# Experts' weights with adjacent rows on each partition, router and filter steps reordered, in a two-block hybrid layer with a mixture of experts

## The reference, cut to what matters

```python
probs = softmax(h @ router_w); sel = probs + router_b
idx = top 2 of sel inside the best of 4 groups of experts
gp = probs[idx] / sum(probs[idx])
for e in range(16):
    he = (silu(h @ w_gate[e]) * (h @ w_up[e])) @ w_down[e]   # 1024x512, 1024x512, 512x1024
    out = out + combine[:, e:e+1] * he
x = x + gate * out
return rmsnorm(x, final_norm_g)
```

## Time and profile before

| | |
|---|---|
| median of 3 runs | 1018.84 us (1018.74 to 1019.75) |
| profiled execution, its own time | 1019.72 us |
| its span | 1017.9 us |
| PE busy | 963.6 us (95%) |
| DVE, ACT, POOL busy | 619.0, 458.8, 53.7 us |
| DMA | 229.71 MB, 226 GB/s over the span |
| mean granted PE clock | 0.987 |

### The profile page before, as it was taken

One profiled execution on the slowest core, in us unless ns is written; L12 is line 12 of the kernel. 1 busy time (PEld: TensorE's weight loads), 2 busy tenths in 40 slices (PEclk: granted clock), 3 DMA queues, 4 the chain that ended last, 5 costly groups with the idle time before them and its releaser, 6 DMA issues.

```text
span 1017.9 us, 14807 instructions
## 1 busy us (share of the span) xinstructions
PE 963.6 (95%) x6088; PEld 743.2 (73%) x6088; DVE 619.0 (61%) x1085; ACT 458.8 (45%) x739; POOL 53.7 (5%) x74
## 2 busy tenths in 40 slices
PE   9989998999998989999989999999799999999994
PEld 6778676778897979999877886899775555544541
DVE  5666639587637476576564899665952545472725
ACT  4576742976645464344653101336640324252402
POOL 0200000000000000000010312000000000010120
PEclk9999999999999999999989999999999999999997
DMA  9933877875342754524461134001799999999992
GB/s 327 246 135 131 280 249 253 290 277 199 132 166 84 272 183 153 180 83 169 165 198 56 67 126 166 1 1 66 274 405 363 404 395 392 409 405 403 399 411 112
DMA packets 111313, 229.71 MB, mean 226 GB/s; under 512 B 8518, under 2 KB 16999, under 8 KB 111246
## 3 DMA queue, kind: packets, MB, share of 16 engines
q1 hardware_dynamic: 107966, 219.40, 59.5%
q0 software_dynamic: 2992, 8.79, 2.2%
q10 hardware_dynamic: 288, 0.58, 0.2%
HBM read 221.01 MB, written 7.74 MB: 225 GB/s over the span
## 4 chain that ended last, share of the span: by engine, by line
PE 65%; DVE 21%; ACT 6%; DMA 4%; issue 3%; SPq 0%; DVEq 0%; ACTq 0%
PE bank L1731 8%; PE bank L2856 8%; PE bank L1732 7%; PE bank L1733 7%; PE bank L956 5%; PE bank L2802 4%; PE bank L2803 3%; PE bank L2804 3%; PE bank L2880 3%; PE bank L907 3%; DMA slot<-in_moe_w_down 2%; DVE slot_rounded L1721 1%; DMA arena<-in_ctxT 1%; PE bank L1159 1%; DVE slot_rounded L772 1%
## 5 line engine op out<-in xcount | busy, mean ns | idle before, releaser
L1731 PE MATMUL bank<-rounded 128*128 128x256 f32 (+1 forms) x800 | 245.7, 307 | 13.4 <-DVE slot_rounded L1721 5.9
L1732 PE MATMUL bank<-rounded 128*128 128x256 f32 x704 | 199.2, 283 | 0.0
L1733 PE MATMUL bank<-rounded,slot_rounded 128*128 128x256 f32 x624 | 176.8, 283 | 0.0
L1731 PEld LDWEIGHTS bank<-rounded 128*128 128x128 f32 x800 | 152.3, 190 | 32.5 <-issue 16.5
L1732 PEld LDWEIGHTS bank<-rounded 128*128 128x128 f32 x704 | 134.4, 191 | 1.0 <-issue 0.7
L1733 PEld LDWEIGHTS bank<-rounded,slot_rounded 128*128 128x128 f32 x624 | 119.3, 191 | 0.0
L956 PE MATMUL bank<-x_and_h,slot 128*128 128x256 f32 x416 | 93.7, 380 | 1.4 <-ACT x_and_h L652 1.4
L1721 DVE TENSOR_TENSOR slot_rounded<-slot,rounded 128x1024 fp32r<-128x1024 f32 (+1 forms) x72 | 74.1, 1052 | 32.1 <-ACT rounded L1715 31.9
L956 PEld LDWEIGHTS bank<-x_and_h,slot 128*128 128x128 f32 x416 | 77.8, 190 | 13.2 <-issue 3.0
L1715 ACT ACTIVATE rounded<-slot 128x1024 fp32r<-128x1024 f32 (+1 forms) x72 | 63.3, 908 | 25.1 <-PE bank L1733 25.1
L1010 ACT ACTIVATE arena<-bank 128x256 f32<-128x256 f32 x56 | 21.5, 385 | 99.2 <-PE bank L956 69.6
(11 more groups left out here) (511 smaller groups left out, 1926.3 us busy)
## 6 DMA issues: line engine op xcount, KB each, us to landing
slot<-in_w_in SPq DMA_DIRECT2D x26, 2048.0 KB, 8.4
slot<-in_ada_w SPq DMA_DIRECT2D x12, 2048.0 KB, 8.4
slot<-in_moe_w_down SPq DMA_DIRECT2D x10, 2048.0 KB, 18.3
more_slots<-in_moe_w_gate SPq DMA_DIRECT2D x8, 2048.0 KB, 15.7
more_slots<-in_moe_w_up SPq DMA_DIRECT2D x8, 2048.0 KB, 18.6
slot<-in_moe_w_gate SPq DMA_DIRECT2D x7, 2048.0 KB, 12.0
more_slots<-in_moe_w_down SPq DMA_DIRECT2D x5, 2048.0 KB, 17.1
x_and_h<-in_moe_w_up SPq DMA_DIRECT2D x5, 2048.0 KB, 15.2
```

The lines of the kernel that those rows point to most:

```text
L1731: t.do.matmul(dst, w_hi, x_hi, start=start, stop=False)
L1732: t.do.matmul(dst, w_hi, x_lo, start=False, stop=False)
L1733: return t.do.matmul(dst, w_lo, x_hi, start=False, stop=stop)
```

## The change

Weights: a partition now holds 8 adjacent rows of a gate or up matrix (4 of a down matrix), 16 KB in one run of DRAM, where it held rows 128 apart. Channel `c` then sits on partition `c // 8`, place `c % 8`, so tokens are put in that order: transposes and gathers take every eighth column of the token tiles as the stationary operand, `turn` every fourth of the hidden rows, and a quad's gate and up products read every fourth column of the weights. Gain and shift are put in that order by a PE transpose and a trip through DRAM (`gain_turn`). Order: ranks are turned by a PE product, compared, and multiplied with the token numbers on PE. Gathers of the first quarter start with token tile 0, and the second half of `tokens_low` moves behind `onehot(0)`; ACT's first `split`s and DVE's third `gathered` change places with their neighbours. Filter: layer 0 one channel job earlier, and two channel jobs more between layer 1 and the taps; POOL's cast waits for the last angle, the ones are filled by DVE. Attention: `weigh` behind `cmp_keys`, one `mix` behind `ada` 6. Tail: the first token tile's picks are added ahead of the last two blocks' rows; the fetch of the second tile and the final row wait for the last weights; squares by halves; the second half's gain and root in one operation.

```diff
-        PLAN += [*channels("f0")[0:2], *woven([*channels("f0")[2:], *channels("f1"), *channels("q2")], taps)]
+        PLAN += [pf0[0], pf0[1], taps[0], pf0[2], pf0[3], taps[1], pf1[0], pf1[1], *woven([*pf1[2:], *pq2], taps[2:])]
+        for job, behind in ((("weigh", ("slc", 0, 1)), ("cmp_keys",)), (("mix", ("slc", 0, 0)), ("ada", 6))):
+            PLAN.remove(job)
+            PLAN.insert(PLAN.index(behind) + 1, job)
...
             g.wait_ge(*at("masks_in"))
+            g.wait_ge(*at("filter_turns", 1))
             g.do.tensor_copy(masks, wide_masks).then_inc(*inc("masks"))
-            for i in range(2):
-                g.do.memset(pk[i], 1.0).then_inc(*inc("pk_ones", i))
...
         def vector_hg_start(v):
+            for i in range(2):
+                v.do.memset(pk[i], 1.0).then_inc(*inc("pk_ones", i))
...
+            t.do.transpose(bank[0:2 * KT, 0:P], mods[:, 24:40, 0], ident[:, :]).then_inc(*inc("gain_turned"))
...
+            g.do.dma_start(gain_dram.rearrange("h (q p) -> (h q) p", p=P), gain_rows).then_inc(*dma("gain_written"))
+            g.wait_ge(*at("gain_written"))
+            g.do.dma_start(gain_by_row, gain_dram.rearrange("h (p j) -> p h j", j=KT)).then_inc(*dma("gain_back"))
...
+        x_hi_spread, x_lo_spread = (x[:, :, :].rearrange("p t (c k) -> p t k c", k=KT) for x in (x_hi, x_lo))
...
-        w_dram = [d["moe_w_" + n].rearrange("e (k p) n -> p (e k) n", p=P) for n in ("gate", "up", "down")]
+        w_dram = [d["moe_w_" + n].rearrange("e (p k) n -> p e (k n)", p=P) for n in ("gate", "up", "down")]
...
-                        mm = t.do.transpose(banks[i][:, k % 2 * S + tt * P:k % 2 * S + (tt + 1) * P], x_normed[:, tt, k * P:(k + 1) * P], ident[:, :])
+                        mm = t.do.transpose(banks[i][:, k % 2 * S + tt * P:k % 2 * S + (tt + 1) * P], x_spread[:, tt, k], ident[:, :])
...
+                        if n == 4:
+                            t.wait_ge(*at("moe_rank"))
+                            t.do.matmul(banks[5][0:16, 32:48], rank, ident[:, 0:16], start=True, stop=True).then_inc(*inc("moe_rank_turned"))
...
+                for first in (0, KT // 2) if c == 0 else ():
+                    four = range(first, first + KT // 2)
+                    for k in four:
...
+                        t.do.matmul(banks[bank][:, 0:CHUNK], x_hi_spread[:, 0, k], slot_onehot[:, 0, cols], start=True, stop=False)
...
+                        if KIND[b] == "quad":
+                            w = weights[i // 2][:, k, :].rearrange("p (c f) -> p f c", f=4)[:, i % 2 * 2:i % 2 * 2 + 2]
...
+                by_place = here[:, 0:S].rearrange("p (k c) -> p k c", c=P) if KIND[b] == "quad" else here.rearrange("p (c k) -> p k c", k=4)
...
             for tt in range(NT):
+                if tt == NT - 1:
+                    g.wait_ge(*weights_loaded(VISITS[-1], DOWN))
...
+            a.wait_ge(*at("gain_back"))
...
-                if c in (1, 2):
-                    split(c - 1)
...
+                    split(0)
+            split(1)
...
+            tokens_low(0)
...
-            v.do.tensor_tensor(by_rank, compared.rearrange("p e r -> p r e"), bcast(expert_row, 1, 16), ALU.mult).then_inc(*inc("router_steps"))
-            v.wait_ge(*now("router_steps"))
-            v.do.tensor_reduce(order, by_rank, AX_X, ALU.add).then_inc(*inc("router_steps"))
-            v.wait_ge(*now("router_steps"))
-            v.do.tensor_copy(order_i, order).then_inc(*inc("moe_order"))
+            tokens_low(1)
             onehot(1)
...
+            gathered(2)
             in_order_low(0)
-            gathered(2)
             in_order_low(1)
...
+            picked_before = {("rows", len(BLOCKS) - 2): (0, 0), ("rows", len(BLOCKS) - 1): (0, 1)}
             for job in EXPERT_JOBS:
+                if job in picked_before:
+                    rows_picked(*picked_before[job])
...
+            s.wait_ge(*weights_loaded(VISITS[-1], DOWN))
             s.do.dma_start(final_row, d["final_row"].to_broadcast([P, D])).then_inc(*dma("final_row_in"))
```

More of the change, by code:

```diff
@@ L268, in build @@
             same("mods_here", 96)
+            same("gain_here", P + 2 * KT)
             homes_r, at_word = {}, 0
@@ L522, in build @@
                  ("hg_close",), g2[0], g2[1], ("cat_split", "hy"), ("cat_split", "fn"), g2[2], g2[3], ("cat_split", "hg")]
-        PLAN += [("router_fold",), ("out2", 0), *[job for k in range(KT - 1) for job in (("out2", k + 1), ("x_turn", k))], ("x_turn", KT - 1)]
+        PLAN += [("router_fold",), ("out2", 0), ("gain_turn",), *[job for k in range(KT - 1) for job in (("out2", k + 1), ("x_turn", k))], ("x_turn", KT - 1)]
         PLAN.insert(PLAN.index(("cmp_turn", 1)) + 1, ("h1_split",))
@@ L2070, in vector_hg_set @@
                 v.wait_ge(*at("masks"))
-                for i in range(2):
-                    v.wait_ge(*at("pk_ones", i))
+                v.wait_ge(*now("pk_ones"))
                 v.wait_ge(*now("hg_start"))
@@ L2426, in build, with tensor_gain_turn, scalar_gain_turn, gpsimd_gain_turn @@
         h3_gain, h3_shift = mods[:, 32:40, 0], mods[:, 24:32, 0]
+        gain_dram = nc.dram_tensor("gain_in_order", (2, D), F32, kind="Internal").ap()
+        @part(TENSOR, "gain_turn")
+        def tensor_gain_turn(t):
+            bank = psum.take(t, ("gain_turn",))
+            t.wait_ge(*at("router_fold", "gain"))
+            t.do.transpose(bank[0:2 * KT, 0:P], mods[:, 24:40, 0], ident[:, :]).then_inc(*inc("gain_turned"))
+            psum.give(bank, ("gain_rows",))
+        @part(SCALAR, "gain_turn")
+        def scalar_gain_turn(a):
+            a.wait_ge(*at("gain_turned"))
+            a.do.activation(gain_rows, psum.of["gain_turn",][0:2 * KT, 0:P], ACT.Copy).then_inc(*inc("gain_rows"))
+        @part(GPSIMD, "gain_turn")
+        def gpsimd_gain_turn(g):
+            g.wait_ge(*at("gain_rows"))
+            g.do.dma_start(gain_dram.rearrange("h (q p) -> (h q) p", p=P), gain_rows).then_inc(*dma("gain_written"))
+            g.wait_ge(*at("gain_written"))
+            g.do.dma_start(gain_by_row, gain_dram.rearrange("h (p j) -> p h j", j=KT)).then_inc(*dma("gain_back"))
         x_mean, x_root, x_scratch = x_stat[:, 2], x_stat[:, 3], x_stat[:, 4]
@@ L2490, in build @@
         one2, share, slot, slot_in_memory = M.take(4, 2), M.take(2, NT), M.take(2, NT), M.take(2, NT)
-        key, rank, base, order = (M.take(16) for _ in range(4))
-        whole = M.take(16)
+        key, rank, base = (M.take(16) for _ in range(3))
+        placed = M.take(16)
         order_i, slot_i = M.take(16).bitcast(I32), M.take(2, NT).bitcast(I32)
-        y_sums, y_mean, y_root, y_scratch = (M.take(NT) for _ in range(4))
+        y_mean, y_root, y_scratch = (M.take(NT) for _ in range(3))
+        y_sums = M.take(2, NT)
         arena_lifetime.close()
@@ L2517, in build @@
         h3_high = sb("tokens_in_order_high", [P, KT * S], F32R)[:, :]
+        h3_shift_here, h3_gain_here = gain_by_row[:, 0], gain_by_row[:, 1]
         h3_low_flat, h3_high_flat = h3_r, h3_high
@@ L2524, in build @@
         slot_row = w_slots[5][:, 0:n_gathered]
-        compared, by_rank, by_expert = (w_slots[5][:, 2048 + 256 * i:2304 + 256 * i].rearrange("p (a b) -> p a b", a=16) for i in range(3))
+        compared, by_expert = (w_slots[5][:, 2048 + 256 * i:2304 + 256 * i].rearrange("p (a b) -> p a b", a=16) for i in range(2))
+        rank_is = w_slots[5][0:16, 2560:2576]
         gate_row = [rms[:, 0:2, :].rearrange("p a s -> p (a s)"), sb("gate_row", [P, W])[:, :]]
@@ L3022, in scalar_experts @@
             for tt in range(NT):
-                a.wait_ge(*at("x3", tt))
-                a.do.activation(by_quarter(y_squares), x_tok[:, tt], ACT.Square,
-                                accum_out=y_sums[:, tt:tt + 1]).then_inc(*inc("y_sums", tt))
-                a.wait_ge(*now("y_sums"))
+                for half in range(2):
+                    x = slice(2 * half, 2 * half + 2)
+                    a.wait_ge(*(at("x3", tt) if half else at("x3", "first", tt)))
+                    a.do.activation(y_squares[:, tt, x], x_tok[:, tt, x], ACT.Square,
+                                    accum_out=y_sums[:, half, tt:tt + 1]).then_inc(*inc("y_sums", tt, half))
             a.wait_ge(*at("y_mean"))
             a.do.activation(y_root, y_mean, ACT.Abs_reciprocal_sqrt).then_inc(*inc("y_root"))
-            a.wait_ge(*at("y_final_root"))
-            a.do.activation(picked[0][:, 0, :], picked[0][:, 0, :], ACT.Copy, scale=y_mean[:, 0:1]).then_inc(*inc("y_first"))
+            a.wait_ge(*at("y_gained"))
+            a.wait_ge(*at("final"))
+            a.do.activation(picked[0][:, 0, :], picked[0][:, 0, :], ACT.Copy, scale=y_root[:, 0:1]).then_inc(*inc("y_first"))
         def vector_experts(v):
@@ L3101, in vector_experts @@
             v.wait_ge(*now("router_steps"))
-            v.do.tensor_reduce(rank, compared, AX_X, ALU.add).then_inc(*inc("router_steps"))
+            v.do.tensor_reduce(rank, compared, AX_X, ALU.add).then_inc(*inc("moe_rank"))
```

(1 more changed line is left out.)

114 lines of the change are left out of this document (70 added, 44 removed).

## The result

The changed kernel takes 1039.21 us (median of 4 runs, 1039.10 to 1039.55) beside 1018.79 for the kernel before: a ratio of 1.0188, interval 1.0163 to 1.0214. It is 20.4 us slower, where 14.85 us faster was forecast, and it lies outside the range. Its span is 1037.5 us, 19.6 longer.

A forecast was written before the change was run, and what follows sets the result against it. PE, busy 95% of the span, was taken as the bound; −2.3 − 6.3 + 0.15 − 1.5 − 2.2 − 2.7 = −14.85 took 1018.84 to 1004.0 us. Likeliest case 1000 to 1008; 8-in-10 range 999.5 to 1019.

The forecast's parts named there:

- Strided reads on PE: Gathers, transposes, turns and quads: cost taken as 0; far end +9.0 gathers, +6.3 turns, +9.3 quads.
- rival 2: Strided stationary and moving operands both cost 1.64 ns per element: +24.6, 1028.6 us, slower than before; chance 0.11.
- The rule of the Trainium skill: SBUF reads: two hits per 16-byte line needed for full speed, so float32 steps of 4 or 8 fall below it.
- rivals 1 and 2: Rival 1: strided weight loads slow PE's gathers and turns, 1017 to 1019.3 us, chance 0.15; rival 2 adds moving operands, 0.11.
- Attention, -2.3: Sparse attention: keys ready earlier, −1.0, and mix behind an ada job fills a wait, −1.3; bounds 0 to −2.8.
- Filter, -6.3: Filter: pause for the second sine goes, −3.4, and half clock behind it, −0.9 and 2.0; bounds 0 to −6.5.
- the 2.9 us for the clock: Filter: without the pause, first taps gain 0.9 and 21 projection products some 2.0 by avoiding the half clock.
- Router and gathers, -1.5: Router and gathers: shorter DVE way to onehot(0), −0.8, and gathered(2) brought forward, −0.7; bounds 0 to −2.8.
- Weights, -2.2: Experts: longer DRAM runs and 4 us of lead remove both PE waits for weights; bounds 0 to −2.2.
- Tail, -2.7: After PE's last product: earlier picks −2.0, one gain and halved squares −0.6, dropped copy −0.1; bounds −0.5 to −3.7.
- The reserve of 0.6 for the second tile's fetch: Tail: 0.6 us kept back because the second tile's fetch now waits for the last weights.
- rival 4: New layout doesn't help transfers, and long runs could delay POOL's small transfers for the picks: +3, 1007 us; chance 0.06.

The follow-up runs named there:

- natural: Changed kernel with the old layout, no gain and shift trip, all edits of order kept; 1014.81 us, ratio 0.9946 to the kernel before.
- layout_alone: Kernel before with only the new layout and the trip of gain and shift, in the old order; 1046.76 us, ratio 1.0240.
- steps: Kernel before, old layout, PE reading with steps of 1, 2, 4 and 8 float32; gather quarters 3.8 us at step 2, 7.73 at step 8.
- mixed_att_old: mixed with the attention's weigh and mix in their old places; 1010.61 us, ratio 0.9900 to the kernel before.
- mixed: Changed kernel, but ACT writes tokens in the gathers' order and down matrices keep the old layout; gate and up in 16 KB runs; 1010.77 us, ratio 0.9900.
- mixed_filter_old: mixed with the filter's layers, cast and fills as in the kernel before; 1015.43 us, ratio 0.9933 to the kernel before.
- mixed_again: The kernel of mixed once more, beside pairs on the same chip; 1011.40 us, ratio 0.9911 to the kernel before.
- pairs: Changed kernel with two adjacent gate/up rows per partition (4 KB runs, PE token step 2), down in the old layout, ACT doing nothing; 1009.48 us, ratio 0.9883.

## Why the prediction was wrong, point by point

- **Strided reads on PE, taken at 0: this step failed.** The prediction put the pace of DVE's strided row aside because it is of another engine, and took the end of the range that costs nothing. The runs show 2.0 times the pace for gathers and quads. In the changed kernel the gathers' stretch is 12.1 us longer; natural, with adjacent reads, gains 1.4 there, so steps cost 13.5. Quads: three times 3.8, so 11.4; turns 3.2; transposes 0.1. Sum 28.2, against the 24.6 of rival 2. Between the forecast and the measured span lie 34.4 us: these 28.2, then 4.3 of clock and 2.2 of attention (both below), and small terms of either sign. Rival 2 had the mechanism, both operands, and fell short in price. It had 9.0 for the gathers, at a ratio of 1.76 where it is 2.0; that 2.6 of it would hide in waits was nearly right (natural still waits 1.7 and 0.4 us there, and the changed kernel doesn't). For the quads it had 9.3. There it took 6 groups of 3.66 where there are three, one group being gate and up together, and took off a cover that it didn't work out; the three cost 11.4 with nothing covered. Turns it had at 6.3 (72 × 0.09 is 6.5), twice too high. The text said that this far end goes into the range, but the range ended at 1019 and rival 2 stood at 1028.6. layout_alone and steps show the cost by itself.
- **The rule of the Trainium skill** (page and section as above) was given no part in the sum. Its two hits in a line of 16 bytes held for the reads in question: free or nearly so at a step of 2, full price at 4 and at 8. The DVE row, at a step of 16, could not show a threshold. The chance of 0.15 and 0.11 for rivals 1 and 2 was too low.
- **Attention, -2.3: wrong, -0.1.** PE's waits of 1.5, 0.4 and 1.3 became 0.5 and 2.6. What ends last is DVE's chain to the turned table (L1469 at 172.22 before, L1475 at 171.82 after): it came 0.4 earlier only. The `ada` job ahead of the mix took 3.46 instead of 1.92, behind the longer wait, with a clock of 0.66 from 170 to 175 us. mixed_att_old measures no difference against mixed. The prediction read each wait by itself and not the chain that feeds both.
- **Filter, -6.3: right in mechanism, 5.8 by the shifts and some 3 to 5 by mixed_filter_old.** In the latter's profile the clock is at 0.50 from 529 to 532 us only, where the kernel before had it there from 525 to 530 and some 2 us more around it, so part of the 2.9 us for the clock depends on the run. That run undoes the cover, the cast's wait and the fills together, so what each is worth by itself isn't shown.
- **Clock elsewhere, not forecast: +4.3 in the changed kernel's profile** (+2.6 before 364 us and +1.7 before 601). No part of the change stands there. Much the same shifts, +2.6 at 364 and then +1.7 at 601, stand in layout_alone, whose first 670 us are those of the kernel before; steps, with the old order too, is 2.8 later at 364; and mixed and mixed_again, the same kernel, differ by 2.0 us at 364. Of the twelve other profiles eleven are 1.2 to 2.9 us later there than that of the kernel before, so it is this profile that was a lucky one. The clock falls behind other pauses in other runs. What decides it stays open.
- **Router and gathers, -1.5: right where steps don't hide it** (natural's shift goes from -4.9 at the token transposes to -6.3 at the shares, -1.4). A new wait of 1.2 us for ACT's `gate_row`, in natural too, limits the gathers' start.
- **Weights, -2.2: right, some -1.9.** Without steps, the experts' stretch is 1.9 shorter in mixed and 2.0 in pairs. (In the changed kernel its parts are 11.4 + 3.2 - 2.2 + 0.4 = 12.8, where 11.8 was measured; 1.0 stays unexplained.) The first weights are issued at 712.55, where it was 717.93. Both waits are gone with 16 KB and with 4 KB runs for gate and up, and stay (2.0 and 1.0) in natural, where only the lead was gained. So it is the length of the run of DRAM, not the lead.
- **Tail, -2.7: 2.6.** The reserve of 0.6 for the second tile's fetch was the right doubt: with late weights 1.5 is lost there.
- `gain_turn` was hidden, as forecast: no wait for it stands in the changed kernel, and natural, without it, starts its gathers as late behind the transposes.

## What to carry to other kernels

Look at what each strided operand hits in 16 bytes before a layout is turned round: here a step of 2 float32 was free or nearly so and a step of 4 or 8 doubled loads and streams, so a layout that helps DMA should leave PE at least two neighbours, as the one of pairs does. Price both ends of an unknown cost by what it would do to the whole sum; an assumption of nothing on 216 loads and 192 products outweighed all the gains that were worked out with care. A wait that is taken from the engine that waits comes back if the chain that feeds it is not shortened.

## What the runs showed of the hardware

- Gather products with a stationary operand of 128 columns (4 bytes each): 0.12 us at steps 1 and 2, 0.24 at steps 4 and 8. Moving operands of 256 float32 columns, 64 products in four column groups: 3.66 us at step 1, 3.9 at step 2, 7.43 at step 4.
- The 16 token transposes hardly pay (1.94 to 2.03 for step 8; their weight loads take 193 ns instead of 140), though they load as many strided columns as a gather product whose load goes from 189 to 338 ns. Why a transpose's load is so much cheaper stays open.
- ACT pays a factor of 2.0 for reads and 1.6 for writes with a step of 8, DVE 1.7 for reads.
- Gate and up matrices with 16 KB runs landed in 9.4 to 15.6 us in mixed (medians by buffer, without the one that is used once), with 2 KB runs in 14.0 to 19.3 in natural; 4 KB runs, at 10.0 to 17.3 in pairs, were enough to end PE's waits.
- Beside 16 KB runs POOL's small transfers of result rows land later, the half of rival 4 that came true: in the changed kernel those of 32 KB in 8.1 us (4.6 before), those of 512 KB in 12.2 (6.6 before). In pairs, with 4 KB runs, they take 4.9 and 7.8. In the changed kernel DVE waited 3.0 us for one of them, PE for none.
